# Eight fixed experts in two quads, one wide first gather, and a second layer norm per column block

## The chip, the cores and the metric

The kernel runs on one core of a Trainium2 chip. The metric is the device time of one launch in microseconds. The engines of a core run side by side, each with its own queue of instructions: TensorE (matmuls, transposes), VectorE, ScalarE, GpSimd, and SyncE, which here issues nearly all DMAs. They wait for each other by semaphores.

## The reference, cut to what matters

One layer of a decoder for 256 prompt positions and 8 sample rows, 264 tokens of 2048 features in fp32. Two mixers (a diagonal state-space one and a gated linear recurrence) give h; the change lies behind them:

```python
h = layer_norm(ALPHA * x + merged @ w_o, ln1_g, ln1_b)
# per token: best of 4 groups, then the best 2 of the 8 experts of that group
hid = silu(tok @ w_g[e]) * (tok @ w_u[e]) * combine[:, e]     # 2048 -> 256, 32 experts
moe = sum over e of hid @ w_d[e]                              # 256 -> 2048
ple = sigmoid(h @ w_pg) * (p @ w_pp)
x_new = layer_norm(ALPHA * h + moe + ple, ln2_g, ln2_b)
```

All 32 experts' weights, some 200 MB, have to be read once; each expert sees about 16 of the 264 tokens.

## The kernel before, in words

Up to about 960 us the kernel computes the mixers and h. Then comes the expert stage, where the change is. Tokens sit on partitions in three tiles of 128, 128 and 8 rows (`TOK`), accumulated in `atok`.

**Groups.** An expert pass is a *group* of four experts with 32 token slots each (a quad) or two experts with 64 each (a pair). `PLANS[0]` lists nine groups: the fixed quad 0 to 3, four quads, two pairs, two quads. Numbers from `FIXED` on are places in an order made at run time: experts sorted by their token count, with the four fullest of the others in the pairs (`order_of_experts`). SyncE reads that order into registers before it can address such an expert. If an expert has more tokens than slots, a flag starts four more rounds of pairs (the branch at `more > 0`).

**Blocks.** `BLOCKS` joins groups that are gathered together. A gather multiplies the tokens (`hH`, `hL`, `hS`, a split of h in two fp32r parts) by 0/1 selections (`selm`, `sels`, written by `select` on VectorE) and leaves the chosen tokens' features in `Xg`: eight units (`u`) of two feature steps, 128 columns for one group, 256 for two. The first block's gather (`first_gather`, line 940) is special: it reads the unsplit fp32 `htok`, and its units stand between the weight steps of group 0 as `FIRST_GATHER` says. ScalarE scales each unit into `Xg`. Block 1 is gathered behind the last weight step of group 0, each later block in the steps of the group before it.

**One group on TensorE.** `gate_up` (line 974) has four weight steps `s`; between them stand scatters of the group two before, gather units, the selection's turn (`slots`), and PLE slices (`PLE_AT`: four column blocks of the PLE gate and projection, each with one group). Then come `down` of the group before and the turn of the hidden values. `scatter` brings expert outputs back to tokens; VectorE adds them to `atok` (`scatter`, line 2396), after ScalarE and VectorE have split them into `outh` and `outl` (lines 1529 and 2404). `REST_AT` names the group with which ALPHA * h is added.

**The weight ring.** `mslot` has ten slots of 1 MB. SyncE loads pieces in the order in which TensorE uses them (`gate_up_load`, `down_load`); `slot_free` (line 1141) makes the load of piece c wait until piece c - 10 is used. Loads of gate and up weights are two DMAs of 512 KB to a slot, down weights one DMA of 1 MB.

**The end.** After the last group's down and all its scatters, VectorE takes the branch, and then for the tiles in `NORM_ORDER` = small, first, second takes statistics (line 2480), mean, deviation and scalars; ScalarE normalises; gain and bias, loaded before that as two full tiles `ln2`, are applied by VectorE (lines 2498 and 2500) or, for the small tile, by GpSimd (lines 1305 and 1307); SyncE stores each tile in one piece. Nearly all matmuls carry line 518, that of the helper `mm`.

Of the kernel before, what the change touches and what calls it, by code (L numbers as in the profile page):

```python
# [23 lines left out]
P = 128  # L24
# [19 lines left out]
BLOCKS = [[[0], [1, 2], [3, 4], [5, 6], [7, 8]]] + [[[2 * b, 2 * b + 1] for b in range(len(PAIRS) // 2)]] * 4  # L44
PLE_AT = {2: 0, 3: 1, 4: 2, 7: 3}
# [53 lines left out]
def build(nc, t, outs):  # L99
# [155 lines left out]
    ln2 = at("ln2", R_Z + 24576, [P, 2, D])  # L255

# [41 lines left out]
    over = at("over", o + 5696, [P, 6])  # L298
    ln1 = const("ln1", [P, 2, KD])
# [10 lines left out]
    with ExitStack() as ctx:  # L310
        def sem(name):
# [44 lines left out]
        gained, small_gain = sem("gained"), sem("small_tile_gain")  # L356
# [18 lines left out]
        final_vectors = sem("final_vectors_there")  # L375
        f_var, f_sq, f_nmr, f_norm = (sem("final_variance"), sem("final_deviation"), sem("final_scalars"),
                                      sem("final_normalized"))
        f_small, f_out = sem("final_small_tile_ready"), sem("final_ready")
# [86 lines left out]
        def down_done(eng, rnd, g, h):  # L465

            eng.wait_ge(m_used, m_at["d", rnd, g, h, len(PLANS[rnd][g]) - 1] + 1)

# [32 lines left out]
        def _(pe):  # L501
# [438 lines left out]
            def first_gather(u):  # L940

                b = side(("ga", 0, 0, u))
                if u == 0:
# [3 lines left out]
                sel = [selm[:, 0, 0, 0:128].bitcast(F32), selm[:, 0, 1, 0:128].bitcast(F32),  # L947
                       sels[0:NB, 0, 0:128].bitcast(F32)]
# [58 lines left out]
            def down(rnd, g):  # L1007
# [4 lines left out]
                for h in range(2):  # L1012
# [3 lines left out]
                    for q in range(2):  # L1016
                        nb = 2 * h + q
                        banks_free(nb)
                        for j in range(2):
                            for i in range(ne):  # L1020
                                rows = slice(width * i, width * (i + 1))
                                last = mm(bank[nb][rows, :], hidT[:, j, rows],
                                          mslot[slot[i] % RM][:, j * 1024 + q * 512:j * 1024 + (q + 1) * 512],
# [1514 lines left out]
```

## Time and profile before

| | us |
|---|---|
| median of 3 runs | 1590.06 |
| lowest, highest | 1585.72, 1596.23 |
| profiled execution | 1587.91 |
| its span | 1586.0 |

| engine | busy us | share of the span |
|---|---|---|
| TensorE, matmuls | 1421.7 | 90% |
| VectorE | 763.3 | 48% |
| ScalarE | 341.4 | 22% |
| GpSimd | 95.8 | 6% |

Over the span the core moved 353 MB by DMA, of which 227 MB after 930 us. Busy shares are averages over stages with different limits: the stage of the mixers reads little and is bound by TensorE, the expert stage reads most of the bytes. The time between engines is read from the rows further down.

### The profile page before, as it was taken

The page shows a single profiled execution, that of the slowest core. Times are in us where ns is not written, and L with a number is a line of the kernel's source. Part 1 is how long each engine was busy: PE and PEld are TensorE (multiplying, and loading weights), DVE is VectorE, ACT ScalarE, POOL GpSimd, SP SyncE. Part 2 cuts the span into 40 slices and gives each one's busy share as a digit, 9 for nine tenths or more (in the row PEclk, how much of TensorE's full clock was granted, in tenths as well). Part 3 has the DMA queues.
Part 4 walks back from the last instruction along what each step waited for, and adds up shares of the span by engine and source line. Part 5 has one row for each costly group of instructions (what it writes and reads, how often), then busy time and mean ns, then how long its engine had stood idle before and what let it go on. Part 6 is the DMA issues. An engine that isn't in the chain of part 4 may idle for free.

```text
span 1586.0 us, 21185 instructions
## 1 busy us (share of the span) xinstructions
PE 1421.7 (90%) x8709; PEld 1079.3 (68%) x8709; DVE 763.3 (48%) x1506; ACT 341.4 (22%) x480; POOL 95.8 (6%) x96
## 2 busy tenths in 40 slices
PE   6969999999999999998999997966989899799971
PEld 4968998777778678767999996522747474356320
DVE  3749877888874336314567446311121303220437
ACT  3423232000010010003334334231211121111102
POOL 3730000000010100000010000100000000000002
PEclk9979999999999789978999997888999999899986
DMA  8425444333333432333565464799999999999991
GB/s 219 155 82 160 158 146 147 107 106 107 106 115 115 137 108 99 119 126 94 181 194 180 157 235 147 301 391 407 385 340 403 408 389 348 409 389 404 409 371 56
DMA packets 139103, 353.25 MB, mean 223 GB/s; under 512 B 20676, under 2 KB 21788, under 8 KB 138480
## 3 DMA queue, kind: packets, MB, share of 16 engines
q1 hardware_dynamic: 135944, 341.99, 59.8%
q0 software_dynamic: 3056, 9.83, 2.1%
q8 instruction: 71, 1.16, 0.3%
q14 instruction: 32, 0.26, 0.0%
HBM read 344.61 MB, written 7.18 MB: 222 GB/s over the span
## 4 chain that ended last, share of the span: by engine, by line
PE 79%; DMA 9%; DVE 7%; issue 2%; ACT 1%; SPq 1%; DVEq 0%; ACTq 0%
PE bank L518 77%; DMA mslot<-in_w_exp_up 5%; DMA mslot<-in_w_exp_down 3%; DVE atok L2396 1%; SPq L1183 1%; DVE lo L1604 1%; PE bank L533 1%; ACT hi L1330 1%; DMA stS<-in_state_hgrn 1%; DMA ident<-in_consts 1%; DVE stS L1926 0%; DVE stats L2480 0%; DVE outl L2404 0%; DVE nmr L2492 0%; DVE ws L1773 0%
## 5 line engine op out<-in xcount | busy, mean ns | idle before, releaser
L518 PE MATMUL bank<-XT,raw 128*128 128x264 f32 x1280 | 309.3, 402 | 0.0
L518 PEld LDWEIGHTS bank<-XT,raw 128*128 128x128 f32 x1280 | 250.5, 198 | 47.3 <-issue 3.2
L1604 DVE TENSOR_TENSOR lo<-raw,hi 128x2048 fp32r<-128x2048 f32 x68 | 159.0, 2339 | 133.9 <-ACT hi L1330 133.9
L1330 ACT ACTIVATE hi<-raw 128x2048 fp32r<-128x2048 f32 x68 | 130.2, 1914 | 236.0 <-PE bank L518 232.9
L518 PE MATMUL bank<-mslot,Xg 128*32 128x512 f32 (+1 forms) x1024 | 147.1, 664 | 31.0 <-DMA mslot<-in_w_exp_up 29.8
L518 PE MATMUL bank<-XH,hi 128*128 128x264 f32 x512 | 148.9, 291 | 7.4 <-DVE lo L1604 6.2
L518 PE MATMUL bank<-XL,hi 128*128 128x264 f32 x512 | 147.2, 287 | 0.0
L518 PE MATMUL bank<-XH,lo 128*128 128x264 f32 x512 | 146.2, 286 | 0.0
L518 PEld LDWEIGHTS bank<-mslot,Xg 128*32 128x32 f32 (+1 forms) x1024 | 39.7, 124 | 115.2 <-issue 114.4
L518 PE MATMUL bank<-HT,mslot 128*128 128x264 f32 x512 | 116.5, 387 | 0.0
L518 PEld LDWEIGHTS bank<-HT,mslot 128*128 128x128 f32 x512 | 96.5, 190 | 18.0 <-issue 1.7
L518 PEld LDWEIGHTS bank<-XH,hi 128*128 128x128 f32 x512 | 98.0, 191 | 8.7 <-issue 4.8
L518 PE MATMUL bank<-mslot,hidT 128*32 128x512 f32 (+1 forms) x512 | 74.1, 674 | 30.2 <-DMA mslot<-in_w_exp_down 29.9
L518 PEld LDWEIGHTS bank<-XL,hi 128*128 128x128 f32 x512 | 98.0, 191 | 0.0
L518 PEld LDWEIGHTS bank<-XH,lo 128*128 128x128 f32 x512 | 97.8, 191 | 0.0
L2396 DVE TENSOR_TENSOR atok<-atok,bank 128x512 f32<-128x512 f32 (+1 forms) x108 | 66.7, 673 | 64.5 <-PE bank L518 64.5
L2427 DVE SCALAR_TENSOR_TENSOR hid<-bank,combg,gsil 128x256 f32<-128x256 f32 x9 | 4.4, 484 | 154.1 <-ACT gsil L1533 153.9
L518 PEld LDWEIGHTS bank<-mslot,hidT 128*32 128x32 f32 (+1 forms) x512 | 20.9, 125 | 79.1 <-issue 78.9
L518 PE MATMUL bank<-MH,hi 128*128 128x264 f32 x256 | 73.1, 286 | 0.0
L518 PE MATMUL bank<-ML,hi 128*128 128x264 f32 x256 | 72.8, 284 | 0.0
L518 PE MATMUL bank<-MH,lo 128*128 128x264 f32 x256 | 72.4, 283 | 0.0
L2404 DVE TENSOR_TENSOR outl<-bank,outh 128x512 fp32r<-128x512 f32 x36 | 23.7, 680 | 73.5 <-ACT outh L1529 73.4
(409 smaller groups left out, 2245.0 us busy)
## 6 DMA issues: line engine op xcount, KB each, us to landing
raw<-in_w_in SPq DMA_DIRECT2D x72, 1024.0 KB, 5.1
mslot<-in_w_exp_gate SPq DMA_DIRECT2D x128, 512.0 KB, 10.1
mslot<-in_w_exp_up SPq DMA_DIRECT2D x128, 512.0 KB, 12.1
mslot<-in_w_exp_down SPq DMA_DIRECT2D x64, 1024.0 KB, 14.9
raw<-in_w_out SPq DMA_DIRECT2D x16, 1024.0 KB, 5.0
mslot<-in_w_ple_gate SPq DMA_DIRECT2D x16, 1024.0 KB, 15.0
raw<-in_w_branch_b SPq DMA_DIRECT2D x8, 1024.0 KB, 5.0
raw<-in_w_branch_a SPq DMA_DIRECT2D x8, 1024.0 KB, 5.1
```

The source lines that it names most:

```text
L518: return nc.tensor.matmul(out, w, x, start=start, stop=stop)
L533: last = nc.tensor.transpose(b[:, t0:t0 + tn], xtok[0:tn, tt, k * 128:(k + 1) * 128], ident[0:tn, 0:tn])
L1183: sp.dma_start(dst.rearrange("p (k f) -> p k f", k=4), src[:, 4 * s:4 * s + 4, :]).then_inc(m_land[c % RM], 16)
L1330: nc.scalar.activation(hi[:, s % RH, :], raw[:, n % RD, :], ACT.Copy).then_inc(hi_done, 1)
L1604: v.tensor_tensor(lo[:, n % RD, :], raw[:, n % RD, :], hi[:, s % RH, :].bitcast(F32), ALU.subtract).then_inc(lo_done, 1)
L2396: v.tensor_tensor(atok[0:tn, tt, cs], atok[0:tn, tt, cs], b[0:tn, :], ALU.add).then_inc(read, 1)
L2404: v.tensor_tensor(outl[:, nb % 2, :], bank[nb][:, :], outh[:, nb % 2, :].bitcast(F32), ALU.subtract).then_inc(out_low, 1)
L2427: v.scalar_tensor_tensor(out=hid[:, :], in0=bank[4][:, FE:2 * FE], scalar=combg[:, g % 2:g % 2 + 1], in1=gsil[:, :], op0=ALU.mult, op1=ALU ...
```

## The change

There are now eight fixed experts, 0 to 3 and 4 to 7, in the first two quads; the places after them hold the pairs (8 to 11) and the quads (12 to 31). The plan is: two fixed quads, two quads, two pairs, three quads. Block 0 is both fixed quads, so `first_gather` makes 256 columns; the last block is one quad. Block 1 is gathered within group 1. PLE slices go with groups 2, 3, 6 and 7 instead of 2, 3, 4 and 7. The choice within the group of experts is one multiply and one reduce.

The down weights of the last group come in three pieces (columns of two blocks, one, one), and TensorE scatters a piece's blocks before it goes on to the next. VectorE takes the statistics per column block between these scatters. Gain and bias are loaded as eight rows of 512 (`ln2row`) and spread over the partitions by TensorE and ScalarE in the last group (`norm_rows`). In the final norm the deviations of all tiles are aggregated together, with one Sqrt on ScalarE and one reciprocal; the rest is on VectorE alone, in halves of 1024 columns into `ynorm`, in the order first, second, small tile, with half-tile stores for the first two, and it stands before the branch instead of after it.

```diff
-FIXED = 4
-WIDE = 8
+FIXED = 8
+WIDE = 12
-PLANS = [[list(range(FIXED))] + QUADS[:4] + PAIRS[2:4] + QUADS[4:]] + [PAIRS] * 4
-BLOCKS = [[[0], [1, 2], [3, 4], [5, 6], [7, 8]]] + ...
-PLE_AT = {2: 0, 3: 1, 4: 2, 7: 3}
+PLANS = [[[0, 1, 2, 3], [4, 5, 6, 7]] + QUADS[:2] + PAIRS[4:6] + QUADS[2:]] + [PAIRS] * 4
+BLOCKS = [[[0, 1], [2, 3], [4, 5], [6, 7], [8]]] + ...
+PLE_AT = {2: 0, 3: 1, 6: 2, 7: 3}
...
+        def pieces(rnd, g):
+            return ((0, 2), (2, 3), (3, 4)) if (rnd, g) == (0, len(PLANS[0]) - 1) else ((0, 2), (2, 4))
...
             def first_gather(u):
-                        last = mm(b[:, q * 256:q * 256 + 128], htok[0:tn, tt, ks], sel[tt], tt == 0, tt == 2)
+                        last = mm(b[:, q * 256:(q + 1) * 256], htok[0:tn, tt, ks], sel[tt], tt == 0, tt == 2)
...
 def down, on TensorE
-                for h in range(2):
+                for h, (n0, n1) in enumerate(pieces(rnd, g)):
+                    if after is not None and h:
+                        for nb in range(*pieces(rnd, g)[h - 1]):
+                            after(nb)
...
 def expert_round, on TensorE
-                        if nxt is not None and (rnd, g) != (0, 0):
+                        if nxt is not None:
                             gather(rnd, nxt, 2 * s)
                             gather(rnd, nxt, 2 * s + 1)
...
-                        if (rnd, g, s) == (0, 0, 3):
-                            for u in range(8):
-                                gather(rnd, nxt, u)
+                        if (rnd, g, s) == (0, groups - 1, 3):
+                            norm_rows(0)
...
-                down(rnd, groups - 1)
-                for nb in range(4):
-                    scatter(rnd, groups - 1, nb)
+                down(rnd, groups - 1, lambda nb: scatter(rnd, groups - 1, nb))
+
+            def norm_rows(again):
+                pe.wait_ge(ln2_ld, 32)
+                for r in range(8):
+                    b = side(("row", again, r))
+                    mm(b[:, :], ident[0:8, r:r + 1].to_broadcast([8, 128]), ln2row[:, :], True, True).then_inc(
+                        misc_ready, 1)
...
 SyncE, in the last group before its downs
+                    if rnd == 0 and g == len(plan) - 1:
+                        sp.wait_ge(misc_ready, misc["ple", 3, 2][0] + 1)
+                        for i, n in enumerate(("ln2_gain", "ln2_bias")):
+                            sp.dma_start(ln2row[4 * i:4 * i + 4, :], t[n][0].rearrange("(r n) -> r n", r=4)).then_inc(
+                                ln2_ld, 16)
-                gate_up_done(sp, rnd, len(plan) - 1)
-                for i, n in enumerate(("ln2_gain", "ln2_bias")):
-                    sp.dma_start(ln2[:, i, :], t[n].to_broadcast([P, D])).then_inc(ln2_ld, 16)
...
 GpSimd
-            nc.gpsimd.tensor_tensor(small_y, small_y, ln2[0:NB, 0, :], ALU.mult).then_inc(small_gain, 1)
-            nc.gpsimd.tensor_tensor(small_y, small_y, ln2[0:NB, 1, :], ALU.add).then_inc(f_small, 1)
...
 experts_of_tokens (VectorE)
-                for g in range(GROUPS):
-                    link(v.tensor_tensor(dst[:, :, :], le, w, ALU.mult))
-                    if g:
-                        link(v.tensor_tensor(ing[:, :, :], ing[:, :, :], ctmp[:, :, :], ALU.add))
+                link(v.tensor_tensor(inall[:, :, :].rearrange("p t (g e) -> p t g e", g=GROUPS),
+                                     logit[:, :, 4:36].rearrange("p t (g e) -> p t g e", g=GROUPS),
+                                     oh[:, :, :].unsqueeze(3).to_broadcast([P, 3, GROUPS, EPG]), ALU.mult))
+                settle()
+                link(v.tensor_reduce(ing[:, :, :], inall[:, :, :].rearrange("p t (g e) -> p t e g", g=GROUPS), AX_X,
+                                     ALU.add))
...
 VectorE, the end
+            def row_statistics(nb):
+                for tt, (t0, tn) in enumerate(TOK):
+                    final_link(v.bn_stats(stats[0:tn, tt, nb, :], atok[0:tn, tt, nb * 512:(nb + 1) * 512]))
+
+            def last_give_back(g):
+                store(0, g, 0)
+                store(0, g, 1)
+                scatter(0, g, 0)
+                scatter(0, g, 1)
+                row_statistics(0)
+                store(0, g, 2)
+                row_statistics(1)
+                scatter(0, g, 2)
+                store(0, g, 3)
+                row_statistics(2)
+                scatter(0, g, 3)
+                row_statistics(3)
+
+            def final_norm(again):
...
+                for tt, (t0, tn) in enumerate(TOK):
+                    for step in range(2):
+                        for half in range(2):
+                            cs = slice(1024 * half, 1024 * (half + 1))
+                            if step == 0:
+                                v.scalar_tensor_tensor(out=ynorm[0:tn, tt, cs], in0=atok[0:tn, tt, cs],
+                                                       scalar=mv[0:tn, tt, 0:1], in1=ln2[0:tn, 0, cs],
+                                                       op0=ALU.subtract, op1=ALU.mult).then_inc(gained, 1)
+                            else:
+                                v.scalar_tensor_tensor(out=ynorm[0:tn, tt, cs], in0=ynorm[0:tn, tt, cs],
+                                                       scalar=rstd[0:tn, tt:tt + 1], in1=ln2[0:tn, 1, cs],
+                                                       op0=ALU.mult, op1=ALU.add).then_inc(f_out, 1)
...
             expert_round(0)
+            final_norm(0)
             dve.wait_ge(flag_ready, 1)
             more = dve.value_load(flag[0:1, 0:1], min_val=0, max_val=1)
```

## Rows read from the trace of the kernel before

**Rows 1.** The page: mean busy share of DMA in 40 slices, in tenths.
```profile
DMA  8425444333333432333565464799999999999991
```

**Rows 2.** The page: the chain that ended last, by engine.
```profile
PE 79%; DMA 9%; DVE 7%; issue 2%; ACT 1%; SPq 1%; DVEq 0%; ACTq 0%
```

**Rows 3.** Stretches: length, busy by engine (instructions), PEclk, DMA share, GB/s.
```profile
979.30:990.60 11.30, 11.23 (x40) 8.57 (x40) 9.25 (x27) 2.95 (x5) 0.00 (x0) 0.50 0.00 0
990.60:995.50 4.90, 4.90 (x34) 1.17 (x33) 0.00 (x0) 0.81 (x2) 0.00 (x0) 0.73 0.01 3
995.50:999.70 4.20, 4.20 (x28) 3.24 (x32) 0.00 (x0) 0.81 (x2) 0.00 (x0) 1.00 0.63 198
...
1003.30:1005.30 2.00, 2.00 (x19) 1.76 (x19) 0.00 (x0) 0.00 (x0) 0.00 (x0) 1.00 1.04 358
1005.30:1015.20 9.90, 9.90 (x37) 7.49 (x36) 1.35 (x14) 1.61 (x4) 5.30 (x3) 0.58 1.02 410
...
1026.60:1036.30 9.70, 9.70 (x85) 9.69 (x82) 9.05 (x5) 7.56 (x15) 0.00 (x0) 1.00 1.02 391
...
1152.00:1168.00 16.00, 16.00 (x106) 9.58 (x104) 1.73 (x4) 1.56 (x4) 0.00 (x0) 1.00 0.81 267
...
1304.00:1324.00 20.00, 20.00 (x126) 12.87 (x125) 1.73 (x4) 2.85 (x5) 0.00 (x0) 1.00 0.85 296
...
1015.00:1022.00 7.00, 7.00 (x49) 3.04 (x47) 6.55 (x5) 1.98 (x8) 0.00 (x0) 0.85 0.66 241
...
1080.00:1100.00 20.00, 12.34 (x68) 3.50 (x69) 1.29 (x2) 1.36 (x3) 0.00 (x0) 0.74 1.03 407
...
1520.00:1526.50 6.50, 6.50 (x33) 1.68 (x34) 0.00 (x0) 0.00 (x0) 0.00 (x0) 0.56 1.03 411
```

**Rows 4.** Timeline of TensorE, start and length: first gather and third weight step.
```profile
979.37 1.19 PE L518 MATMUL bank<-selm,htok 128*128 128x128 f32 x4 [1.94 <-DVE sels L2196]
...
1015.21 4.55 PE L518 MATMUL bank<-mslot,Xg 128*32 128x512 f32 x32
```

**Rows 5.** The same, a PLE slice; an fp32 matmul shows as two instructions.
```profile
1270.59 7.28 PE L518 MATMUL bank<-HT,mslot 128*128 128x264 f32 x32
```

**Rows 6.** Timeline of VectorE: router and first selection.
```profile
970.35 0.18 DVE L2057 TENSOR_TENSOR ing<-logit,oh 128x24 f32<-128x24 f32 x1
...
971.88 0.30 DVE L2063 MAX8 emx<-ing 128x8 f32<-128x8 f32 x3
...
978.29 0.43 DVE L2192 TENSOR_TENSOR selm<-iota,rank 128x256 fp32r<-128x256 f32 x1
```

**Rows 7.** Timeline of the tail; in brackets idle time before and its releaser.
```profile
1499.26 6.57 PE L518 MATMUL bank<-mslot,Xg 128*32 128x512 f32 x32 [3.23 <-DMA mslot<-in_w_exp_up]
...
1509.69 3.64 PE L518 MATMUL bank<-mslot,hidT 128*32 128x512 f32 x32 [2.41 <-DMA mslot<-in_w_exp_down]
...
1519.93 6.47 PE L518 MATMUL bank<-mslot,hidT 128*32 128x512 f32 x32 [6.59 <-DMA mslot<-in_w_exp_down]
...
1537.12 3.64 PE L518 MATMUL bank<-mslot,hidT 128*32 128x512 f32 x32
...
1541.63 1.29 DVE L2404 TENSOR_TENSOR outl<-bank,outh 128x512 fp32r<-128x512 f32 x2 [3.34 <-ACT outh L1529]
...
1545.34 1.87 DVE L2396 TENSOR_TENSOR atok<-atok,bank 128x512 f32<-128x512 f32 x3 [2.41 <-PE bank L518]
...
1557.77 0.68 DVE L2480 BATCH_NORM_STATS2 stats<-atok 8x6 f32<-8x512 f32 x1 [3.99 <-issue]
...
1563.60 4.49 POOL L1305 TENSOR_TENSOR atok<-atok,ln 8x2048 f32<-8x2048 f32 x1 [551.40 <-ACT atok L1577]
...
1564.62 3.48 DVE L2492 SCALAR_TENSOR_TENSOR nmr<-mv,rstd 128x1 f32<-128x1 f32 x1
...
1572.61 2.28 DVE L2498 TENSOR_TENSOR atok<-atok,ln 128x2048 f32<-128x2048 f32 x1
...
1572.69 9.41 SPq L1224 DMA_DIRECT2D out<-atok  x3
```

More of the change, by code:

```diff
@@ L437, in ple_places @@
                 m_size.append(16)
+        def pieces(rnd, g):
+            return ((0, 2), (2, 3), (3, 4)) if (rnd, g) == (0, len(PLANS[0]) - 1) else ((0, 2), (2, 4))
         def down_places(rnd, g):
-            for h in range(2):
+            for h in range(len(pieces(rnd, g))):
                 for i in range(len(PLANS[rnd][g])):
@@ L1005, in gate_up, with down @@
                     between(s)
-            def down(rnd, g):
+            def down(rnd, g, after=None):
                 ne = len(PLANS[rnd][g])
@@ L1015, in down @@
                         m_landed(pe, slot[i])
-                    for q in range(2):
-                        nb = 2 * h + q
+                    for nb in range(n0, n1):
                         banks_free(nb)
@@ L1021, in down @@
                                 rows = slice(width * i, width * (i + 1))
+                                at_ = (j * (n1 - n0) + nb - n0) * 512
                                 last = mm(bank[nb][rows, :], hidT[:, j, rows],
-                                          mslot[slot[i] % RM][:, j * 1024 + q * 512:j * 1024 + (q + 1) * 512],
-                                          j == 0, j == 1)
-                                if q == 1 and j == 1:
+                                          mslot[slot[i] % RM][:, at_:at_ + 512], j == 0, j == 1)
+                                if nb == n1 - 1 and j == 1:
                                     last.then_inc(m_used, 1)
+                if after is not None:
+                    for nb in range(*pieces(rnd, g)[-1]):
+                        after(nb)
                 downs[0] += 1
@@ L1186, in down_load @@
                 def down_load(g):
-                    for h in range(2):
+                    for h, (n0, n1) in enumerate(pieces(rnd, g)):
                         for i in range(len(plan[g])):
@@ L1547, in expert_round @@
                     nxt = next_block(rnd, g)
-                    early = 6 if nxt is not None and (rnd, g) != (0, 0) else 0
+                    early = 6 if nxt is not None else 0
                     if g >= 2:
@@ L1563, in expert_round, with norm_rows @@
                 store(rnd, groups - 1)
+            def norm_rows(again):
+                for r in range(8):
+                    b, read = side(("row", again, r))
+                    if r == 0:
+                        gate_up_done(act, *((4, len(PLANS[4]) - 1) if again else (0, len(PLANS[0]) - 1)))
+                    nc.scalar.activation(ln2[:, r // 4, (r % 4) * 512:(r % 4 + 1) * 512], b[:, :],
+                                         ACT.Copy).then_inc(read, 1)
+            def final_norm(again):
+                act.wait_ge(f_var, again + 1)
+                nc.scalar.activation(rstd[:, :], rstd[:, :], ACT.Sqrt).then_inc(f_sq, 1)
             expert_round(0)
+            nc.scalar.activation(warm[:, :], ones[:, 0:1], ACT.Sqrt)
+            final_norm(0)
             act.wait_ge(flag_ready, 1)
@@ new lines, in final_norm @@
+            def final_norm(again):
+                dve.wait_ge(tail, done[0])
+                for tt, (t0, tn) in enumerate(TOK):
+                    final_link(v.bn_aggr(mv[0:tn, tt, :], stats[0:tn, tt, :, :].rearrange("p a b -> p (a b)")))
+                dve.wait_ge(tail, done[0])
+                for tt, (t0, tn) in enumerate(TOK):
+                    last = v.tensor_scalar(rstd[0:tn, tt:tt + 1], mv[0:tn, tt, 1:2], LN_EPS, None, ALU.add)
+                    if tt < 2:
+                        final_link(last)
+                last.then_inc(f_var, 1)
+                dve.wait_ge(f_sq, again + 1)
+                final_link(v.reciprocal(rstd[:, :], rstd[:, :]))
+                dve.wait_ge(tail, done[0])
+                for r in range(5, 8):
+                    side_read(dve, ("row", again, r))
+                for tt, (t0, tn) in enumerate(TOK):
+                    for step in range(2):
[5 more added lines that the diff above has]
+                                                       op0=ALU.subtract, op1=ALU.mult).then_inc(gained, 1)
+                            else:
+                                dve.wait_ge(gained, 6 * again + 2 * tt + half + 1)
+                                v.scalar_tensor_tensor(out=ynorm[0:tn, tt, cs], in0=ynorm[0:tn, tt, cs],
+                                                       scalar=rstd[0:tn, tt:tt + 1], in1=ln2[0:tn, 1, cs],
+                                                       op0=ALU.mult, op1=ALU.add).then_inc(f_out, 1)
```

130 lines of the change are left out of this document (51 added, 79 removed).

## The prediction

> **What bounds the kernel now.** The page's slices come first: DMA is at 9 nearly everywhere in the last fifteen slices and mostly between 2 and 5 before [rows 1]. The last 600 us stream the expert weights. The chain of waits gives TensorE most of the span and DMA a tenth [rows 2]; in the expert stage the two are close partners, for the ring of ten 1 MB slots is refilled only as TensorE uses slots. So I read DMA share against TensorE by stretches [rows 3]. A stream that is never short of a free slot shows a share of 1.03 and 410 GB/s, 2.56 us a megabyte; ten slots are 26 us of stock. It falls below that in few places: it stands still while the first gather and the first weight matmuls run (979 to 995), at 1015 to 1022 (7.0 x 0.37/1.03 = 2.5 us), at 1152 to 1168 (3.4 us) and at 1304 to 1324 (3.5 us). The last two are the groups in which TensorE does a block gather and a PLE slice together. What sets the end is thus when the stream starts, its holes, and the tail behind its last pieces.
>
> In the first gather, 128-column matmuls [rows 4], TensorE's granted clock is 0.50 (1.2 GHz) for 11.3 us although it is busy throughout; it goes to 1.00 (2.4 GHz) while the 512-column weight matmuls run, and has a mean of 0.58 in the gather's third stretch [rows 3]. The tail is a chain of TensorE, ScalarE and VectorE [rows 7].
>
> Tokens past an expert's slots would start four more rounds. Counting the reference's router on its inputs gives at most 22 tokens in experts 0 to 7 (32 slots each) and 35 in the fullest other one, which the order puts in a group with 64. No further round runs, before or after.
>
> **Part 1, router.** Seven operations between 970.35 and the MAX8 at 971.88 (1.53 us) become a multiply over 96 columns and a reduce. Such operations cost 0.18 us with 24 columns and 0.43 with 256; I take 0.27 each: -1.0. The first selection doubles from 256 to 512 columns, its two small companions too; by column about +0.5 [rows 6]. The gather starts at 978.9, not 979.4.
>
> **Part 2, first gather of 256 columns.** It is 16 steps of three fp32 matmuls, in stretches of 6, 4 and 6. A step costs 11.23/6 = 1.87 us at half clock and 4.20/4 = 1.05 at full [rows 3]. A 264-column fp32 matmul costs 7.28/16 = 0.455 us at full clock [rows 5], so 256 columns 0.44, a step 1.32 and at half clock 2.65. Bounds for all 16: today's 25.4 us below, 42.4 (all at half) above. Which clock? Stretches of 256 and more columns that are long have full clock (1026.6 to 1036.3, 1304 to 1324), and such matmuls stood at half clock for some 6.5 us at most [rows 3, 7]. I take half clock for the first 6 us, then full, and one short fall after the counting matmuls (1.7 us lost). First stretch: 6/2.65 = 2.3 steps and 3.7 x 1.32 = 4.9, to 989.8; weights 3.64 [rows 7], 993.4 (now 995.4); 5.3 + 3.64, 1002.4; counts 2.0 [rows 3], 1004.4; 7.9 + 1.7 + 3.64, 1017.7 (now 1019.8). DMA moved 1.7 us after the release (4.2 us at 0.63 are 2.6 us of transfer, up to 999.7). Eight megabytes of the first two releases last 20.5 us, to 1015.6, and it resumes at 1019.4 instead of 1021.5. **Stream: -2 us.**
>
> The trace has 11.3 busy us at half clock [rows 3]. The Trainium skill (TensorE: Matmul & The Clock Gate, Part 1) says that a TensorE kept busy is brought to full clock, however small its matmuls. The trace speaks against that for today's gather; for the wide one the page's rule gives the first rival.
>
> **Part 3, gathers and PLE slices in other groups.** The eight gather units behind group 0 (9.5 us, [rows 3]) go to group 1, where TensorE waits for weights anyway: nothing. Their ScalarE copies stand behind the 16 feature scalings there; if the cover of unlanded weights were gone it would cost 2 to 5 us. Four fp32r block gathers become three of 256 columns and one of 128. A gather meets a PLE slice in two groups again (3 and 7, before 2 and 4), so the holes of 3.4 and 3.5 us come again: 0. The 128-column fp32r gather has no row. Below: half the time, -4.8 us; above: the fp32 rate, 80 x 0.22 (0.455 x 128/264) = 17.6 instead of 9.5, +8. Its 80 weight loads stay, so I take the 9.5 of the nearest row: 0. Group 1 now has fixed experts, and SyncE's wait for the order with its value loads goes behind it. It fed no hole: 0.
>
> **Part 4, the tail.** Eight row-broadcast matmuls (512 columns fp32, 0.9 us each, 7.2) come between the last gate-up and the last but one down. That down could start at 1507.3 and waits 2.41 us for its first half and 6.59 for its second [rows 7]. With the rows it starts at 1514.5 and ends its half at 1518.1, still before the second half lands at 1519.9. Cover gone (half clock): 13 us, and +3.6. ScalarE's eight copies run beside them. In return TensorE no longer idles 6.6 us before 1519.9, so the second half should take 3.64 instead of 6.47 us: **-2.8**. Slots held 4.9 us longer are refilled from 1518; the stock lasts to 1525.
>
> From the start T of the last down (1537.1) I lay out VectorE anew, from [rows 7]. Matmuls 3.64, copy and subtractions to T+5.8, first add at T+6.0 (now T+8.2); 6 adds of 0.62, 9.7; statistics of block 0 (3 x 0.62) 11.5; subtraction 12.1; statistics 14.0; 3 adds 15.8; subtraction, held by the fourth block's matmuls, 16.8; statistics 18.6; adds 20.4; statistics 22.3. Aggregates, deviation and reciprocal 2.0, to 24.3. Twelve operations of 1024 columns at 1.12 (half of 2.28 less an overhead) 37.7. Today the branch costs VectorE 3.99 us before the statistics; it moves behind the last operation, beside the last store. The last store takes 3.9 us today (1582.1 to 1586.0, 1 MB); one of 64 KB at most that. So 4.0 for both: T+41.7, against T+48.9, **-7.2**. Part of it is the GpSimd work: while it runs, two 1-column VectorE operations stretch, one to 3.48 us. The last slots are freed at T+3.64 and land some 5 us later; the fourth block needs them at T+14. The 1 MB loads of gain and bias ran behind the weights: 0. The row loads make SyncE wait for a PLE turn of the group before, with the last downs queued behind; that is long past: 0, or +2 if not.
>
> The 512 KB gate and up loads ran at 407 GB/s in a full queue [rows 3]. The Trainium skill (DMA: Bandwidth & Descriptors, Bandwidth) advises at least 1 MiB per DMA, which speaks against the smaller last pieces. The trace shows no loss; with a fifth lost on 4 MB it would be 2.6 us, which the slack above covers.
>
> **Sum.** -2 - 2.8 - 7.2 = -12.0 us against the profiled execution (1587.9 us, span 1586.0): **1576 us**. The median of the three runs shown, 1590.06, is 2.2 above that execution. A measurement of this kernel can tell about 1% from no change: faster is below 1574, slower above 1606.
>
> **Rivals.**
> Full clock almost at once, no fall after the counts: third release 1015, stream -4.5 to -5, sum 1573. For it: long fp32 stretches of 264 columns stay at full clock. Against: the 512-column down of 1519.9 ran 6.47 us at half. 0.25.
> Clock as today: 15.9 us in the first stretch, 4.90, 5.3, 3.64, 2.0, 13.8, 4.55 [rows 4], third release 1029, stream +9, sum 1587. For it: 11.3 busy us changed nothing. 0.10.
> **Slower**: half clock from the start to the third release. 42.4 + 3 x 6.57 + 2.5 = 64.6, release at 1043.5, up to +24. From +12.2 on it outweighs the tail and passes 1590; sum 1588 to 1600, middle 1594. For it: the gather's first 11.3 us wholly and its last 9.9 mostly stood at half clock. Against: full clock came with each weight block. 0.07.
> The 128-column fp32r gather at fp32 rate: +8 in group 7, sum 1584. 0.09.
> Row matmuls at half clock: no -2.8 but +3.6, sum 1582. 0.05.
> The base case has 0.37, its own range 1570 to 1582, a third of it under 1574. For a better or worse outcome than any of these (fewer holes, an unknown wait) stay 0.07.
>
> **Numbers.** 0.12 of the base, 0.17 of the first rival and most of the rest give faster 0.34; slower 0.05, the far end of the slower rival and unknown waits; within 0.61. Range 1567 to 1592, which leaves out about 2 in 10.
>
> **What would show it.** Full clock and steps of 1.3 us in most of the gather; third release near 1018; DMA below 1.0 in groups 3 and 7, some 3.5 us each; the last block gather in 9.5 us; the second half of the last but one down in 3.6 us; last down to end in 42 us; twelve final operations of 1.1. It would be wrong if the gather stayed at half clock, if the final operations took longer, or if a further round ran.

## The result, and the profile after

| | before | after |
|---|---|---|
| median us (runs) | 1591.12 (4) | 1609.89 (4) |
| lowest, highest | 1585.72, 1596.23 | 1606.98, 1613.32 |
| profiled execution, its span | 1587.91, 1586.0 | 1607.62, 1605.8 |

The changed kernel is slower: ratio 1.0112, interval 1.0087 to 1.0138, against a forecast of 1576 and a range up to 1592. The spans differ by 19.8 us. Three entries make it up: the expert stage starts late (+8.6), the last group stands still (+16.4), the end is shorter (-5.2).

The page of the kernel after, PEclk and DMA of its 40 slices; the DMA line answers to [rows 1]:

```profile
PEclk9979999999999799978999995988999999999867
DMA  8425444333343433333564462899999999999952
```

The last two digits of DMA, 5 and 2 where before it had 9 and 1, are the first sign: the stream stops short of the end. PEclk has a 5 in the slice of the first gather.

Stretches of the kernel after, with the columns of [rows 3]:

```profile
979.40:998.30 18.90, 18.86 (x36) 10.03 (x36) 8.13 (x27) 3.64 (x5) 0.00 (x0) 0.50 0.00 1
998.30:1004.60 6.30, 6.30 (x34) 1.40 (x33) 0.00 (x0) 1.02 (x2) 0.00 (x0) 0.56 0.00 0
1004.60:1011.30 6.70, 6.70 (x28) 3.87 (x24) 0.00 (x0) 1.02 (x2) 0.00 (x0) 1.00 0.76 260
1014.90:1027.00 12.10, 12.10 (x58) 7.62 (x54) 1.34 (x14) 2.04 (x4) 5.30 (x3) 1.00 1.01 402
1028.00:1034.00 6.00, 6.00 (x53) 3.46 (x49) 5.97 (x5) 2.42 (x7) 0.00 (x0) 1.00 0.37 111
1236.00:1252.00 16.00, 16.00 (x111) 9.42 (x109) 2.36 (x6) 1.76 (x5) 0.00 (x0) 1.00 0.78 266
1440.00:1472.00 32.00, 32.00 (x209) 21.40 (x202) 3.07 (x7) 4.84 (x10) 0.00 (x0) 1.00 0.86 309
...
1529.00:1549.00 20.00, 20.00 (x63) 6.22 (x65) 0.00 (x0) 4.78 (x8) 0.00 (x0) 0.56 0.14 53
...
1004.60:1507.90 503.30, 454.50 (x2687) 254.60 (x2685) 115.62 (x194) 91.13 (x200) 5.30 (x3) 0.95 0.99 386
```

And its timeline of TensorE, start and length, for the first gather and for the last group:

```profile
979.44 2.04 PE L523 MATMUL bank<-selm,htok 128*128 128x256 f32 x4 [2.50 <-DVE sels L2223]
981.41 1.22 PE L523 MATMUL bank<-sels,htok 8*128 8x256 f32 x2
...
998.33 6.33 PE L523 MATMUL bank<-mslot,Xg 128*32 128x512 f32 x32
1004.59 1.13 PE L523 MATMUL bank<-selm,htok 128*128 128x256 f32 x4
1005.65 0.69 PE L523 MATMUL bank<-sels,htok 8*128 8x256 f32 x2
...
1027.05 3.64 PE L523 MATMUL bank<-mslot,Xg 128*32 128x512 f32 x32
...
1507.86 5.86 PE L523 MATMUL bank<-mslot,Xg 128*32 128x512 f32 x32 [3.72 <-DMA mslot<-in_w_exp_up]
...
1527.58 14.02 PE L523 MATMUL bank<-ln2row,ident 8*128 8x512 f32 x16 [12.40 <-DMA ln2row<-in_ln_bias]
1541.53 9.53 PE L523 MATMUL bank<-mslot,hidT 128*32 128x512 f32 x64
...
1562.09 3.64 PE L523 MATMUL bank<-mslot,hidT 128*32 128x512 f32 x32
```

**The start.** TensorE is busy for 18.9 us at a granted clock of 0.50 (1.2 GHz): six steps of 3.15 us, each of two matmuls over 128 rows (x4) and one over the 8 rows of the small tile (x2). The first weights take 6.33 us more, so the first slots come free at 1004.6, 9.2 us later than in [rows 3]. From there the clock is at 1.00 up to the third release at 1030.6, with steps of 1.69 us. All later holes together cost nothing: from the first release to the last gate-up it is 503.3 us at 386 GB/s (last stretch row), while before it was 1499.26 - 995.4 = 503.9. So the +8.6 us of the last gate-up (1507.86 against 1499.26) is all made ahead of the first release. Once at 1.00, the clock also stayed there through the third block of the gather, 10.1 us with the same share of 8-row matmuls (1016.94 to 1027.05).

**The last group.** TensorE waits 12.40 us for the load of the bias rows, computes the rows for 14.02 us, all at half clock, and only then, at 1541.5, begins the down, whose weights had landed when the stream ran out at 1529. SyncE's queue tells why (start, length of the issue with its wait):

```profile
1494.07 20.54 SPq L1208 DMA_DIRECT2D mslot<-in_w_exp_down  x8
1514.66 0.40 SPq L1225 DMA_DIRECT2D ln2row<-in_ln_gain  x1
1515.11 0.28 SPq L1225 DMA_DIRECT2D ln2row<-in_ln_bias  x1
```

The PLE turn is indeed long past. But the loads stand behind the downs of the group before, and the last of those waits for a slot that only the last gate-up frees, at 1513.7. Then 16 KB queue behind a full ring of weight loads and land after another 12 us. Meanwhile no slot is used: the stream runs out at 1529, and the next 20 us have a share of 0.14. The last down starts at T = 1562.09 (T is the start of the last down, as in the prediction), 25.0 us after [rows 7], of which 8.6 came in with the start.

**The end.** From T to the end it takes 43.7 us, before 48.9. The timeline of VectorE in the final norm:

```profile
1586.06 2.48 DVE L2545 SCALAR_TENSOR_TENSOR ynorm<-atok,mv,ln 128x1024 f32<-128x1024 f32 x2
...
1598.02 2.46 DVE L2550 SCALAR_TENSOR_TENSOR ynorm<-ynorm,rstd,ln 8x1024 f32<-8x1024 f32 x2
```

First final operation at T + 24.0 (forecast 24.3), twelve of them in 14.4 us (forecast 13.4), and 5.3 us to the end (forecast 4.0).

### The profile page after: what moved, and what is told of

Its sections match the earlier page's. It is cut to its first block, busy times and chain, and to the rows that moved or that the text cites. A ratio compares the mean times of both kernels' runs of the same rounds, so it can differ in the third digit from the quotient of the medians.

```text
span 1605.8 us, 21188 instructions
## 1 busy us (share of the span) xinstructions
PE 1448.3 (90%) x8725; PEld 1084.6 (68%) x8725; DVE 761.0 (47%) x1503; ACT 339.3 (21%) x484; POOL 86.7 (5%) x94
## 4 chain that ended last, share of the span: by engine, by line
PE 81%; DMA 8%; DVE 7%; issue 2%; ACT 1%; SPq 1%; DVEq 0%; ACTq 0%
PE bank L523 78%; DMA mslot<-in_w_exp_up 4%; DMA mslot<-in_w_exp_down 2%; DVE atok L2423 1%; DVE lo L1633 1%; PE bank L538 1%; DMA ln2row<-in_ln_bias 1%; DMA stS<-in_state_hgrn 1%; ACT hi L1348 1%; DMA ident<-in_consts 1%; DVE ynorm L2545 0%; SPq L1198 0%; DVE stS L1955 0%; DVE ynorm L2550 0%; DVE stats L2500 0%
## 6 DMA issues: line engine op xcount, KB each, us to landing
mslot<-in_w_exp_gate SPq DMA_DIRECT2D x128, 512.0 KB, 10.5
```

## The experiments

There were three theories for the loss at the start and two for the one in the last group. The start: the 8-row matmuls hold the clock down (A), or the idle time ahead of the gather does (B), or the mostly zero selection does (C). The last group: the place of the row loads in SyncE's queue (A), or row matmuls that would cost as much anyway (B). The runs with a ratio to the kernel before; e5 and e6, which ran once each, follow in their own section:

| run | median us (runs) | ratio to before | interval |
|---|---|---|---|
| e1 rows issued by GpSimd | 1594.78 (10) | 1.0015 | 0.9999 to 1.0030 |
| e2 start undone | 1603.65 (6) | 1.0062 | 1.0033 to 1.0090 |
| e3 both | 1584.91 (10) | 0.9958 | 0.9941 to 0.9975 |
| e4 filled idle time | 1582.31 (6) | 0.9933 | 0.9902 to 0.9963 |
| e7 norm behind the branch | 1585.29 (10) | 0.9955 | 0.9933 to 0.9977 |
| e8 two pieces | 1586.39 (10) | 0.9971 | 0.9951 to 0.9990 |
| e9 wide, padded | 1577.80 (5) | 0.9915 | 0.9887 to 0.9942 |
| e10 wide, rows padded too | 1580.09 (6) | 0.9916 | 0.9886 to 0.9946 |
| e11 narrow, all padded | 1574.17 (6) | 0.9890 | 0.9867 to 0.9912 |
| e12 kernel before, padded | 1578.88 (4) | 0.9910 | 0.9874 to 0.9946 |

The kernel before had medians of 1592.86, 1592.17 and 1593.41 beside these runs. It and several versions spread over some 10 us, and the gather's start moves between about 979 and 987 us, in kernels with the same work ahead of it too (979.65 in e1, 986.05 and 986.47 in e5 and e6). So stretches are compared by their length from the gather's start.

### e1: the row loads leave SyncE's queue

```diff
 SyncE, last group
-                        for i, n in enumerate(("ln2_gain", "ln2_bias")):
-                            sp.dma_start(ln2row[4 * i:4 * i + 4, :], ...).then_inc(ln2_ld, 16)
 GpSimd, after the states are stored
+            pool.wait_ge(misc_ready, misc["ple", 3, 2][0] + 1)
+            for i, n in enumerate(("ln2_gain", "ln2_bias")):
+                pool.dma_start(ln2row[4 * i:4 * i + 4, :], ...).then_inc(ln2_ld, 16)
```

> The changed kernel with one thing altered: the two small loads of gain and bias rows are issued by GpSimd as soon as the last PLE turn of group 7 is done, not by SyncE behind the last but one down's pieces. Theory (the rows land late because they stand behind the weights of a full queue): TensorE's wait for them, 12.4 us in the changed kernel, goes to 0; the eight row matmuls still run at half clock (14 us) and cover no gap, so the last but one down starts near 1529 instead of 1541.5. About 1595 us, 12 below the changed kernel, ratio to before 1.00 to 1.01. Rival (the wait is only where the DMA-bound tail shows up, weights would be waited for instead): the down then waits for its second half and the time stays within 4 us of 1608.

The issue of the loads, timeline of GpSimd:

```profile
1473.19 0.52 POOL L1323 DMA_DIRECT2D ln2row<-in_ln_gain  x1 [449.08 <-PE bank L1042]
```

TensorE in the last group:

```profile
1515.60 10.13 PE L523 MATMUL bank<-ln2row,ident 8*128 8x512 f32 x16
1525.66 9.08 PE L523 MATMUL bank<-mslot,hidT 128*32 128x512 f32 x64
```

The loads go out 41 us earlier and land in 5.0 and 5.3 us, beside a stream of 400 GB/s. The wait is gone, and with it 15.1 us of the median (1594.78, forecast about 1595). Theory A of the last group holds: the place behind the downs made the loss. The edit changes two things at once, the queue and the time of the issue; whether SyncE could have issued the loads early enough between its weight loads was not tried. The Trainium skill (DMA: Bandwidth & Descriptors, Queues, rings and completion order) says that a DMA engine serves its queues in turns; the 5.3 us on a queue of its own, against 12 us behind the full one, agree. The rows now take 10.1 us instead of 14.0 (forecast: still 14): TensorE did not stand still before them, and the granted clock is 1.00 up to 1518.0, then falls, and is 0.50 from 1520.0 on, although TensorE is busy throughout.

### e2 and e3: the start of before, without and with e1

```diff
-FIXED = 8
-WIDE = 12
+FIXED = 4
+WIDE = 8
 PLANS, BLOCKS, PLE_AT: those of the kernel before
-                        last = mm(b[:, q * 256:(q + 1) * 256], htok[0:tn, tt, ks], sel[tt], tt == 0, tt == 2)
+                        last = mm(b[:, q * 256:q * 256 + 128], htok[0:tn, tt, ks], sel[tt], tt == 0, tt == 2)
 e3: the edit of e1 as well
```

> The changed kernel with the start of before: four fixed experts, first gather of 128 columns, blocks, PLE slices and the gather behind group 0 as before; the router's two operations and the whole new tail stay. Theory (the start costs what its first gather costs at half clock, some 9 to 11 us of the stream): third release of slots back at 1019, last gate-up near 1499, about 1598 us, ratio 1.004. Rival (the start costs nothing in the end, since the ring evens it out): within 3 us of the changed kernel, 1607.

> Both of the preceding at once. If the two losses are independent, 1607.6 - 9.5 - 12.4 = 1586, near the kernel before (ratio 0.995 to 1.00): what is left of the tail's gain, 5 us, against the row matmuls at half clock. If they overlap, it is no faster than the better of the two, about 1595.

TensorE in e2, behind the last gate-up:

```profile
1522.87 14.02 PE L523 MATMUL bank<-ln2row,ident 8*128 8x512 f32 x16 [14.41 <-DMA ln2row<-in_ln_bias]
```

TensorE in e3: first weights, last gate-up, rows, the two parts of the down, and the last down:

```profile
990.23 5.37 PE L523 MATMUL bank<-mslot,Xg 128*32 128x512 f32 x32
...
1498.88 5.34 PE L523 MATMUL bank<-mslot,Xg 128*32 128x512 f32 x32 [3.21 <-DMA mslot<-in_w_exp_up]
...
1505.68 10.53 PE L523 MATMUL bank<-ln2row,ident 8*128 8x512 f32 x16
1516.14 8.68 PE L523 MATMUL bank<-mslot,hidT 128*32 128x512 f32 x64
...
1534.92 3.64 PE L523 MATMUL bank<-mslot,hidT 128*32 128x512 f32 x32
```

In e3 the last gate-up is back at 1498.9 (before 1499.26), 519.9 us from the gather's start in both. In e2 it stands at 1502.04, but there the gather began at 985.01, so it is 517.0 us; both are far below the 528.4 of the changed kernel. The wide start thus costs 9.9 us beside early row loads (e1 less e3) and 6.2 beside late ones (the changed kernel less e2), the late row loads 15.1 (the changed kernel less e1) to 18.7 (e2 less e3). By the ratios it is 9 and 8 us for the start, 15 and 17 for the row loads: within the noise the two losses add up. e3 came out as forecast (1586). e2 took 5.7 us more than the 1598 forecast, but the interval of its ratio holds the 1.004 forecast with it. What is left of the change, its tail, gains: e3 is 0.42% faster than before. In its profile the last down starts 2.2 us earlier than before, and from there to the end it is 43.6 us (before 48.9): -7.5 in all against the forecast -10.0.

The third block of the narrow gather shows a fall that the wide one does not have. TensorE in e3, behind the counting matmuls:

```profile
1006.42 0.71 PE L523 MATMUL bank<-selm,htok 128*128 128x128 f32 x4
...
1009.35 1.22 PE L523 MATMUL bank<-selm,htok 128*128 128x128 f32 x4
```

The same four instructions take 0.71 us and then 1.22: the granted clock goes from 1.00 to 0.50 at 1007.5. It does so in e2 too, and over the same block the kernel before has a mean of 0.58 [rows 3]; in the changed kernel, e1 and e4 it stays at 1.00.

### e4: matmuls into the idle time ahead of the gather

```diff
             logits_by_token()
+            pe.wait_ge(acc_read[3], BLK_END)
+            for _ in range(12):
+                mm(bank[3][:, 0:256], XT[:, 0, 0:128], XT[:, 1, 0:256], True, True)
             fixed_counts()
+            for _ in range(3): the same matmul
```

> The first kernel of this call (wide gather, rows by GpSimd) with 15 more fp32 matmuls of 256 columns into a free bank, results unused: 12 in the idle time while the router runs and 3 before the first gather. Theory (the first gather is slow because TensorE comes out of idle time at half clock, and the gather itself does not bring it back): granted clock 1.00 through the gather, steps of 1.7 instead of 3.15 us in the first stretch, its six steps in 10 instead of 18.9 us, weights 3.6 instead of 6.3, third release near 1019 instead of 1030.6; about 11 us less than the kernel without them, near 1584. Rival (the gather pulls the clock down by itself): clock falls within the gather again, gain under 4 us; if the added matmuls run at half clock they delay the gather by up to 5 us.

The edits of e1 are in it. Stretches of e4:

```profile
968.00:977.00 9.00, 8.51 (x49) 7.28 (x50) 6.07 (x47) 8.53 (x8) 0.00 (x0) 1.00 0.59 214
977.00:978.60 1.60, 1.05 (x4) 0.30 (x2) 1.50 (x5) 1.60 (x2) 0.00 (x0) 0.56 0.00 0
978.69:997.58 18.89, 18.89 (x36) 10.01 (x36) 8.10 (x27) 4.89 (x6) 0.00 (x0) 0.50 0.00 1
```

The clock is at 1.00 for 9 us, falls just ahead of the gather, and the gather takes 18.89 us, as without the filling. So with most of the idle time filled this gather is as slow as before; idle time alone is not what keeps it slow. The median, though, is what theory B forecast (near 1584): 12.5 us under e1's, with times from 1576.94 to 1587.07, and the profiled one is the slowest of the six. The mean granted clock of every run is on record: 0.942 over the profiled one, 0.946 to 0.948 over the three quickest. What the gather did in the quicker ones was not seen. The run speaks against B as the whole cause and leaves open that the state of the clock at the gather's start counts too.

### e5 and e6: is it the 8 rows or the data?

```diff
 e5
-                    for tt, (t0, tn) in enumerate(TOK):
-                        last = mm(b[...], htok[0:tn, tt, ks], sel[tt], tt == 0, tt == 2)
+                    for tt, (t0, tn) in enumerate(TOK[:2]):
+                        last = mm(b[...], htok[0:tn, tt, ks], sel[tt], tt == 0, tt == 1)
 e6
-                        last = mm(b[...], htok[0:tn, tt, ks], sel[tt], tt == 0, tt == 2)
+                        last = mm(b[...], htok[0:tn, tt, ks], XT[0:tn, 2 * u + q, 0:256], tt == 0, tt == 2)
```

> The changed kernel with rows by GpSimd, and the third matmul of each step of the first gather (contraction over the 8 sample rows) left out: block 0's features lack the sample tokens. Theory (the 8-row matmuls, a third of the gather, keep TensorE at 0.50 through 18.9 us): the clock goes to 1.00 within 7 us of the gather's start; first stretch about 8 us. Rival (it is not them): six steps at 2.0 us, 12 us, all at 0.50, until the 512-column weight matmuls as now.

> The same kernel, all three matmuls kept, but the moving operand of the first gather is a piece of the dense features XT in place of the 0/1 selection (block 0's features are wrong). Theory A (mostly zero data in the moving operand keeps the clock at half): the clock rises within 7 us, first stretch about 12 us. Theory B (8-row matmuls do it) and rival C (it is fp32 gathers of that shape whatever the data): 18.9 us at 0.50 as now.

Both hold e1's edit. e5 leaves the sample tokens out of the first block's features, and e6 multiplies the tokens by dense data in place of the selection; they took 1577.21 and 1591.89 us, one execution each. TensorE in e5 (the six steps are one row), and below it the gather's two stretches:

```profile
986.05 8.09 PE L523 MATMUL bank<-selm,htok 128*128 128x256 f32 x24 [2.49 <-DVE sels L2222]
994.07 3.64 PE L523 MATMUL bank<-mslot,Xg 128*32 128x512 f32 x32
```

```profile
986.05:991.00 4.95, 4.95 (x12) 3.96 (x13) 4.67 (x11) 2.58 (x3) 0.00 (x0) 0.50 0.00 0
991.00:994.00 3.00, 3.00 (x14) 2.38 (x12) 2.69 (x14) 1.02 (x2) 0.00 (x0) 0.92 0.00 0
```

The same stretch of e6:

```profile
986.47:1005.30 18.83, 18.83 (x36) 10.00 (x36) 8.10 (x27) 3.62 (x5) 0.00 (x0) 0.50 0.00 1
```

Without the 8-row matmuls the clock rises 5 us into the gather, and six steps take 8.1 us instead of 18.9. Had they been taken away with the clock left at half, it would have been 6 x 2.0 = 12. With dense data in place of the 0/1 selection nothing moves: 18.8 us at 0.50. C falls. The two gathers started within half a microsecond of each other (986.05, 986.47), so a later start than in the changed kernel does not by itself bring the clock up.

### e7 and e8: the branch and the pieces

```diff
 e7 (on e3), VectorE and ScalarE
             expert_round(0)
-            final_norm(0)
             dve.wait_ge(flag_ready, 1)
             ...
             with dve.If(more > 0):
                 further rounds
+            final_norm(0)
 e8 (on e3)
-            return ((0, 2), (2, 3), (3, 4)) if (rnd, g) == (0, len(PLANS[0]) - 1) else ((0, 2), (2, 4))
+            return ((0, 2), (2, 4))
```

> The kernel with start undone and rows by GpSimd (1584.9 us), with VectorE's and ScalarE's final norm behind the branch on the flag, as before; the branch's further rounds are not fit for use (they do not run). Theory (VectorE pays about 4 us for the branch before the final aggregates, and nothing hides it): last down to end 43.6 + 3 to 4, about 1588.5. Rival (the 5.0 us between the last operation and the end are themselves the branch, which now moves forward): the end comes 1 to 1.5 us earlier after the last operation, net +2 to +3.

> The same base (1584.9 us) with the last down weights in two pieces as before; statistics still per block between the scatters. Theory (TensorE is off VectorE's chain but for a held subtraction): 0 to +2 us, since the scatters of blocks 2 and 3 no longer wait for a piece in between but those of 0 and 1 still come early. Rival (turns of small pieces cost more than they hide): 1 to 3 us faster than the base.

VectorE in e7 behind the last statistics:

```profile
1561.23 0.50 DVE L2530 BATCH_NORM_AGGREGATE mv<-stats 128x2 f32<-128x24 f32 x3 [2.21 <-issue]
```

The branch is worth 2.2 us in the profile (forecast 3 to 4), and from the last operation to the end it is 5.2 us with it ahead or behind. With two pieces it is 39.8 us from the first subtraction behind the last down to the end, in e3 39.1: the third piece is worth 0.8 us. Neither can be told in the medians (1585.29 and 1586.39 for e3's 1584.91; the intervals overlap e3's).

### e9 and e10: the 8 rows padded to 128, wide start

```diff
 GpSimd, once the area is free
+            nc.gpsimd.memset(htok[:, 2, :], 0.0).then_inc(padded, 1)
 TensorE, the first gather; the small selection in all 128 rows
-                        last = mm(b[...], htok[0:tn, tt, ks], sel[tt], tt == 0, tt == 2)
+                        last = mm(b[...], htok[:, tt, ks], sel[tt], tt == 0, tt == 2)
 e10: the row matmuls as well, ln2row zeroed ahead of its load
-                    mm(b[:, :], ident[0:8, r:r + 1].to_broadcast([8, 128]), ln2row[:, :], True, True)
+                    mm(b[:, :], ident[:, r:r + 1].to_broadcast([P, 128]), ln2row[:, :], True, True)
```

> The changed kernel with rows by GpSimd, and the small tile's matmul of the first gather contracting over all 128 rows (rows 8 to 127 of both operands are zero) instead of 8; the same numbers come out. Theory (8-row contractions keep TensorE at 0.50): clock 1.00 within 7 us of the gather's start, first stretch (six steps) in about 13 us instead of 18.9, third release 38 us after the gather's start instead of 51, so some 12 us less than the 1594.8 of the kernel without padding: about 1583. Rival (what helped when the matmul was left out was the missing time, not the rows): clock stays at 0.50 to the first weight matmuls, time within 3 us of 1594.8.

> The same, and the eight row matmuls also contract over 128 rows (zeros below row 8). Theory: they run at 1.00, about 7.3 us instead of 10 to 14, and the last but one down starts with its first half landed and waits for nothing but its second: 1 to 3 us less, 1581. Rival (they are hidden behind that landing anyway): 0.

TensorE in e9:

```profile
984.19 2.05 PE L524 MATMUL bank<-selm,htok 128*128 128x256 f32 x4 [2.50 <-DVE sels L2226]
...
992.67 1.03 PE L524 MATMUL bank<-selm,htok 128*128 128x256 f32 x4
993.53 0.59 PE L524 MATMUL bank<-sels,htok 128*128 128x256 f32 x2
994.06 3.64 PE L524 MATMUL bank<-mslot,Xg 128*32 128x512 f32 x32
```

Its stretch from the rise of the clock on:

```profile
988.00:993.90 5.90, 5.90 (x28) 5.02 (x27) 4.50 (x20) 2.04 (x4) 0.00 (x0) 0.99 0.01 3
```

The same matmuls with 120 rows of zeros more run at full clock after some 4 us. Six steps take 9.9 us instead of 18.9, and the first weights 3.64 instead of 6.33. A step at full clock is 1.30 us (forecast 1.32), for all three matmuls now take 0.43 us. With the 8-row matmul in the step it was 1.69 even at full clock: 0.62 for the one over 8 rows (1005.65 to 1006.27 above) and 0.53 for each of its two neighbours. The median falls by 17 us from e1's (by the ratios 16; the forecast was 12), with the idle time ahead of the gather unchanged at 2.50 us. So theory A of the start is shown from both sides: take the 8-row matmuls away or fill their rows, and the clock comes up within the gather. Two qualifications stand beside it: a clock already at 1.00 was held through 10.1 us of the same mixture (the changed kernel's third block), and e4's quicker runs stay unexplained.

TensorE in e10:

```profile
1502.62 7.10 PE L524 MATMUL bank<-ln2row,ident 128*128 128x512 f32 x16
1509.66 3.64 PE L524 MATMUL bank<-mslot,hidT 128*32 128x512 f32 x32
1516.26 5.34 PE L524 MATMUL bank<-mslot,hidT 128*32 128x512 f32 x32 [2.96 <-DMA mslot<-in_w_exp_down]
```

The rows take 7.10 us, as the prediction's 7.2, but what they gain TensorE waits out: 2.96 us for the second half of the down. The medians show nothing (ratios 0.9915 and 0.9916; 1 to 3 us had been forecast).

### e11 and e12: the padding without the wide start

```diff
 e11: the kernel after with the start of before (e3), padded as in e10
 e12: the kernel before, only its first gather padded
-                        last = mm(b[:, q * 256:q * 256 + 128], htok[0:tn, tt, ks], sel[tt], tt == 0, tt == 2)
+                        last = mm(b[:, q * 256:q * 256 + 128], htok[:, tt, ks], sel[tt], tt == 0, tt == 2)
```

> Start of before (four fixed experts, 128 columns) with the padded small tile, the new tail, rows by GpSimd and padded. Theory: narrow steps at full clock cost 1.05 us against 1.7, so the third release comes some 5 us earlier than with the padded wide gather, 1576 to 1578, 7 less than the same kernel without padding (1584.9). Rival (128-column matmuls leave the clock at 0.50 also with 128 rows): as before, 1584.

> The kernel before with nothing but the padded small tile in its first gather. Theory: the clock rises in the gather, third release (1019.8) 5 to 8 us earlier, about 1586 against 1592. Rival (128-column steps stay at half clock whatever the rows): no change.

TensorE in e11, the three blocks of first weights:

```profile
983.27 1.20 PE L524 MATMUL bank<-selm,htok 128*128 128x128 f32 x4 [1.94 <-DVE sels L2232]
...
989.59 3.64 PE L524 MATMUL bank<-mslot,Xg 128*32 128x512 f32 x32
...
1005.86 3.64 PE L524 MATMUL bank<-mslot,Xg 128*32 128x512 f32 x32
```

Its stretch that answers to 1015 to 1022 of [rows 3], and the one from first release to last gate-up:

```profile
1005.80:1012.80 7.00, 6.99 (x55) 3.71 (x53) 6.70 (x5) 3.03 (x8) 2.78 (x2) 1.00 1.03 416
...
993.20:1492.60 499.40, 448.76 (x2683) 253.33 (x2680) 116.20 (x194) 91.78 (x200) 6.86 (x6) 0.94 1.01 389
```

The narrow gather profits too, and keeps full clock in its third block. The third release comes 26.2 us after the gather's start (before 40.4, e12 26.5), the hole behind it is gone (share 1.03 for 0.66), and the stretch to the last gate-up is 4.5 us shorter. Padding alone makes the kernel before 0.9% faster (interval 0.5 to 1.3%; its four times lie in two pairs, near 1574 and at 1583 and 1586; about 1586 was forecast). With the new tail it is 1.1% faster (1576 to 1578 us were forecast), the lowest median of all kernels here: 1574.17 against 1593.41 for the kernel before beside it, and 1609.89 for the changed one. That the new tail adds to the padding is not shown, for the intervals of e11 and e12 overlap; nor is a gain of the wide start, for e10, the same kernel with it, has 0.9916 to e11's 0.9890.

## Why the prediction was wrong, step by step

**Part 1, router: held.** The stretch from the first of the changed operations to the MAX8 went from 1.53 to 0.66 us; the selections add 0.56 (idle time 2.50 us ahead of the gather, 1.94 before). The gather starts at 979.44, forecast 978.9, before 979.37; half a microsecond cannot be told from this time's spread.

**Part 2, first stretch: failed.** "I take half clock for the first 6 us, then full" is the step. Measured: half clock for all 18.9 us and most of the first weights, first release 1004.6 for 993.4. The forecast read from long fp32 stretches of 264 columns that wide matmuls raise the clock, and put the half clock of today's gather [rows 3] down to its 128 columns. Those stretches have no matmul over 8 rows; both gathers have one in three, and without the 8-row form the clock came up in either (e5, e9, e12). The row that could have told is the first stretch of [rows 3], 11.3 busy us at 0.50, read by shape (8*128 beside 128*128) and not by width alone. The width entered the sum a second way: a step with the 8-row matmul is 1.69 us at full clock and 3.15 at half, not the 1.32 and 2.65 scaled from a row of matmuls over 128 rows.

The rival "clock as today" came out near: third release 1029 (measured 1030.6), stream +9 (measured +8.6), at a chance of 0.10. Part of that is luck, for two errors nearly cancel: its first stretch was 15.9 us and took 18.9, its third was 13.8 and took 10.1. The fall of the clock after the counts, which both it and the base case had, did not come in the wide gather (1.00 from 1014.9 on; e1 and e4 as well), while e2 and e3, narrow as the kernel before, have it; no run shows why. The slower rival had the first stretch's clock right and the later ones' wrong. The first rival, the rule of the Trainium skill (TensorE: Matmul & The Clock Gate, Part 1) that a TensorE kept busy comes to full clock, is contradicted: 18.86 of 18.90 us busy at 0.50, with back-to-back matmuls, and in e1 a fall to 0.50 under the busy row matmuls. The measurement decides.

**Part 3, holes and the 128-column block gather: zero held.** The holes came in groups 3 and 7 with 16.0 x 0.25/1.03 = 3.9 and 32.0 x 0.17/1.03 = 5.3 us instead of 3.5 each, but from first release to last gate-up the time was unchanged (503.3 against 503.9). The 80 fp32r matmuls took 9.5 us, as taken.

**Part 4, the rows: failed, and this is the larger part.** The sentence is "that is long past: 0, or +2 if not". It looked at the semaphore the loads wait for and not at the queue in front of them and behind them. The downs of the group before hold SyncE until the last gate-up frees a slot, so the loads cannot be issued before 1514.7, whatever they wait for. They then need 12 us through a full ring, TensorE waits, and because TensorE frees no slot the stream itself dries up. It cost 15 to 19 us by the medians (the changed kernel less e1, e2 less e3), 15 to 17 by the ratios. Once the loads are early, the forecast's mechanism is there but smaller: in e3 the two down parts end at 1524.8, 1.6 us before 1526.4, for the -2.8 forecast, and 0.4 of the 1.6 were gained before the last gate-up. The rows are at half clock in part (10.5 us for 7.2). The rival "row matmuls at half clock" priced that at +3.6; it did not cost that, since until the second half lands the rows fill idle time (e10: faster rows only turn into a wait of 2.96 us).

**Part 4, the end: right mechanism, sizes off.** -5.2 for -7.2: twelve operations of 1.20 us, not 1.12 (+1.0), and 5.3 us from the last of them to the end, not 4.0 (+1.3). The prediction took the 3.9 us of a 1 MB store as an upper bound for one of 64 KB, and the runs show that it is none. The branch gave 2.2 us (e7), while 3.99 of idle time before were put down to it.

**The sum.** -12.0 was forecast. With the two failed steps put right, from the profiles, it is +8.6 for the start, +16.4 from the last gate-up to T, -5.2 for the end: +19.8.

**Open.** Why the gather's start moves by some 7 us between executions; what e4's quicker runs did; why the mixture with 8-row matmuls leaves a clock of 1.00 alone in the third wide block and not in the third narrow one; what the 5.2 us behind the last operation consist of (in the changed kernel nearly all bytes of the last store moved before 1602, the span ends at 1605.8); and how many rows are enough, as only 8 and 128 were tried.

## What to carry to other kernels

Before moving a small load, walk the issuing queue: the instruction ahead of it may be waiting for the very work that the load's user stands in front of, and a ring of slots makes such a stall spread to the whole stream. Read matmul stretches by operand shape, contraction rows included: here fp32 matmuls of which a third were over 8 rows left TensorE at 1.2 GHz, and padding them with zeros bought 0.9% of the kernel for one memset. And when one engine is made quicker, find the next arrival first: the padded rows gained nothing because the weights came when they came.

## What the runs showed of the hardware that was not expected

- A stretch with fp32 matmuls over 8 rows among those over 128 stayed at a granted clock of 0.50 although TensorE was busy for 18.86 of 18.90 us; sixteen row matmul instructions over 8 rows stood at 0.50 for 14.02 us when TensorE had stood still before them, and in e1, begun at 1.00, they saw the clock fall to 0.50 after some 4 us although TensorE was busy. With 128 rows throughout the clock went to 1.00 within the first stretch of the gather (e5, e9, e11, e12), and the padded row matmuls stayed at 1.00 for their 7.10 us (e10).
- At full clock a 256-column fp32 matmul took 0.43 us beside others over 128 rows (e9); in steps with one over 8 rows, that one took 0.62 and those over 128 rows 0.53 each.
- A load of 8 KB landed in 5 us on GpSimd's queue beside a stream of 400 GB/s, and in 12 us behind that stream on SyncE's.
- The final operations of 1024 columns took the same on 8 partitions (2.46 us for two) as on 128 (2.47).
